# The gate chain of an RG-LRU layer in two batches of three half tiles instead of three batches of two

## The chip, the cores and the metric

The kernel runs on one core of a Trainium2 chip. The metric is the device time of one execution in microseconds (us). The kernel before took 2811.53 us, the median of three runs (2811.03 to 2813.7).

## The reference

The program is a two-layer decoder trunk in float32 for 1024 tokens of width 1024: RMSNorm, retention mixer, SwiGLU FFN, then RMSNorm, Griffin recurrent block (the LRU), SwiGLU FFN, and a final RMSNorm. The change lies wholly in the recurrent block, of width 1536 in 8 blocks of 192:

```python
gate, u = jnp.split(h @ w_in, 2, axis=-1)
u = conv4(u) + conv_b
r = jax.nn.sigmoid(einsum('bsnc,ncd->bsnd', ub, w_r) + b_r)
i = jax.nn.sigmoid(einsum('bsnc,ncd->bsnd', ub, w_i) + b_i)
log_a = (-LRU_C * softplus(-lam)) * r
a = jnp.exp(log_a)
b = jnp.sqrt(-jnp.expm1(2.0 * log_a)) * (i * u)
_, hs = lax.associative_scan(combine, (a, b), axis=1)      # hs[t] = a[t] hs[t-1] + b[t]
y = hs * jax.nn.gelu(gate)
return y @ w_out
```

## The kernel before

Each matrix product is made of three float32r products (high times high, high times low, low times high), so every operand is split: ACT (ScalarE) or POOL (GpSimd) rounds to the high part, DVE (VectorE) or POOL subtracts to get the low one. PE (TensorE) runs all products one behind the other; a 128x512 product is three matmuls per 128 rows of the contraction.

The LRU runs in four groups (g = 0 to 3) of three column tiles of 128 channels. Within a group there are six **items**: item i is tile i mod 3, half i // 3 of the 1024 tokens (512 tokens). PE makes for each item two PSUM banks, one for r and one for i (`lru_gates`, line 856 on). Tiles 0 and 2 meet two 128-row pieces of the contraction and take 6 matmuls a bank, tile 1 meets three and takes 9. PSUM has eight banks in a ring. PE waits in `free(e)` until the semaphore `psum_free` tells that bank e's last tenant is read, so DVE's count of `psum_free` sets when PE may go on.

The gate chain of a group is written out by hand for two engines:

- ACT, `gate_chain` at line 1190: `gates(i)` makes the two sigmoids out of PSUM (lines 1197 and 1202). `tanh_exp(items)` makes the tanh into `s_buf` (line 1211) and the exp, which is a, in place in `r_buf` (line 1215). `roots` takes the square root in `s_buf` (line 1221). `y_round` rounds the finished y (line 1229). Sigmoid, exp and sqrt stand in different tables, so between them ACT runs an ACT_TABLE_LOAD.
- DVE, `gate_chain` at line 1626: `gated` multiplies u by the i gate (line 1634) and is what counts `psum_free` up by two for an item. `scans` does two multiplications (1642, 1645), the scan over the tokens (1650) and the product with the gelu branch (1655). `y_split` makes the low part of y (1660).

Both go through the items in pairs: (0, 1), (2, 3), (4, 5). `s_buf` has two buffers, `r_buf` four, `i_buf` three.

What PE does right behind a group's gate products: in groups 0, 1 and 2 it is the input product of the next group. Its column tile needs two banks and is two units of 24 matmuls; the first tile wants item 2 of the group before gated, the second item 3, the third item 4. In the last group, g = 3, it is the second half (nh = 1) of group 2's output product, three units k = 0, 1, 2 of eight blocks s = 0 to 7, each block three matmuls. Blocks 0 and 1 want item 2 gated, blocks 2 and 3 item 3, blocks 4 and 5 item 4, blocks 6 and 7 item 5. Behind it comes group 3's own output product, nh = 0 first. Its unit k = 0 wants `y_ready` at 6g + 4, that is four items split, and block s of it wants DVE to have added block s of the product before to the residual (line 1353). In the last group these adds stand inside DVE's gate chain, where `meanwhile(blocks)` is called.

The bookkeeping of PE for these two places is:

```python
def lru_outof(g, u0, base, e0, nh, y_hi, y_lo):
    for k in range(GT):
        j = nh * 3 + k
        if nh == 0:
            pe.wait_ge(y_ready, g * 6 + k + 4)
        cols_unit(j, u0 + j, k, GT, y_hi, y_lo, k * S, e0, base)
```

POOL meanwhile splits weights, one unit of 128x512 at a time (`split`, lines 435, 444 and 446), each released when PE begins a unit. After the LRU come the second FFN and the end of the kernel, which take PE's whole time as well.

Of the kernel before, what the change touches and what calls it, by code (L numbers as in the profile page):

```python
# [8 lines left out]
ACT = mybir.ActivationFunctionType  # L9
# [107 lines left out]
def build(nc, x, positions, mix_norm, ffn_norm, final_norm, ret_w_in, ret_w_out, lru_w_in, lru_conv_w,  # L117
# [3 lines left out]
    with ctx:  # L121
# [110 lines left out]
        def t(i):  # L232
            return T[:, i * 512:(i + 1) * 512]

        def r3(i, n=1):
            return R3[:, i * 512:(i + n) * 512]
# [2 lines left out]
        spare = [xn[:, c:c + 512] for c in (GT * S, GT * S + 512, 4096 + GT * S)]  # L239
        r_buf = (t(0), r3(6), dk[:, 0:512], spare[0])  # L240
        i_buf = (t(1), spare[1], spare[2])
        s_buf = (r3(7), t(2))


        x_in = [sem(f"x_in{i}") for i in range(SB)]
# [657 lines left out]
        def _(act):  # L903
# [286 lines left out]
            def gate_chain(g, base, e0, y_hi):  # L1190
                def gates(i):

                    tile = i % GT
                    if i >= 4:
                        act.wait_ge(l_scan, 6 * g + i - 3)
                    full(base + e0 + 2 * i)
                    nc.scalar.activation(r_buf[i % 4], bank(e0 + 2 * i), ACT.Sigmoid,
                                         bias=gc_gate[:, 15 + tile:16 + tile]).then_inc(r_sig, 1)
                    full(base + e0 + 2 * i + 1)
                    if i >= 3:  # L1200
                        act.wait_ge(psum_free, base + e0 + 2 * i - 4)
                    nc.scalar.activation(i_buf[i % 3], bank(e0 + 2 * i + 1), ACT.Sigmoid,
                                         bias=gc_gate[:, 18 + tile:19 + tile]).then_inc(i_sig, 1)

                def tanh_exp(items):

                    for i in items:
                        if i >= 2:
                            act.wait_ge(l_scan, 6 * g + i - 1)
                        act.wait_ge(r_sig, 6 * g + i + 1)  # L1210
                        nc.scalar.activation(s_buf[i % 2], r_buf[i % 4], ACT.Tanh,
                                             scale=gc_gate[:, 21 + i % GT:22 + i % GT]).then_inc(r_tanh, 1)
                    for i in items:
                        act.wait_ge(r_tanh, 6 * g + i + 1)
                        nc.scalar.activation(r_buf[i % 4], r_buf[i % 4], ACT.Exp,
                                             scale=gc_gate[:, i % GT:i % GT + 1]).then_inc(a_exp, 1)

                def roots(items):

                    for i in items:  # L1220
                        nc.scalar.activation(s_buf[i % 2], s_buf[i % 2], ACT.Sqrt).then_inc(t_root, 1)

                def y_round(items):
                    for i in items:
                        act.wait_ge(y_out, 6 * g + i + 1)

                        act.wait_ge(psum_full, base + e0 + (6 if i < GT else 12))
                        at = i % GT * S + i // GT * 512
                        nc.scalar.activation(y_hi[:, at:at + 512], R3[:, at:at + 512], ACT.Copy)\
                            .then_inc(y_rounded, 1)  # L1230

                act.wait_ge(gc_ready, g + 1)
                gates(0)
                gates(1)
                tanh_exp((0, 1))
                roots((0, 1))
                gates(2)
                gates(3)
                y_round((0, 1))
                gates(4)  # L1240
                gates(5)
                tanh_exp((2, 3))
                roots((2, 3))
                tanh_exp((4, 5))
                y_round((2, 3))
                roots((4, 5))
                y_round((4, 5))

            u_round(0, JB_LRU, a_hi)
            gelu(0, JB_LRU, 6)  # L1250
# [26 lines left out]
        def _(dve):  # L1277
# [348 lines left out]
            def gate_chain(g, y_hi, y_lo, meanwhile=lambda blocks: None):  # L1626
# [9 lines left out]
                def scans(items):  # L1636
                    first = step.now()
                    for j, i in enumerate(items):
                        dve.wait_ge(a_exp, 6 * g + i + 1)
                        dve.wait_ge(t_root, 6 * g + i + 1)  # L1640

                        step.up(STT(s_buf[i % 2], r_buf[i % 4], 1.0, s_buf[i % 2], ALU.add, ALU.mult))
                    for j, i in enumerate(items):
                        dve.wait_ge(dve_step, first + j + 1)
                        step.up(TT(uc[:, cut(i)], uc[:, cut(i)], s_buf[i % 2], ALU.mult))
                    for j, i in enumerate(items):
                        dve.wait_ge(dve_step, first + j + 3)
                        tile, hf = i % GT, i // GT
                        start = uc[:, tile * S + 511:tile * S + 512] if hf else 0.0
                        k = nc.vector.tensor_tensor_scan(uc[:, cut(i)], r_buf[i % 4], uc[:, cut(i)], start,  # L1650
# [12 lines left out]
                link(take(gc_gate, g))  # L1663

                TS(gc_gate[:, 0:3], gc_gate[:, 21:24], -2.0, None, ALU.mult).then_inc(gc_ready, 1)
                gated((0, 1))
                scans((0, 1))
                gated((2, 3))
                y_split((0, 1))
                gated((4, 5))  # L1670
                scans((2, 3))
                meanwhile((0, 1))
                y_split((2, 3))
                meanwhile((2, 3))
                scans((4, 5))
                meanwhile((4,))
                y_split((4, 5))
                meanwhile((5, 6, 7))

            per_turn = 1 + 3 * 3 + 1 + 6 * 2  # L1680
# [88 lines left out]
```

## Time and profile before

| | |
|---|---|
| median of three runs | 2811.53 us (2811.03 to 2813.7) |
| profiled execution, its own time | 2815.13 us |
| its span, first to last instruction | 2813.3 us |
| mean granted TensorE clock | 0.985 |
| PE busy | 2712.8 us, 96% of the span |
| DVE busy | 1344.8 us, 48% |
| ACT busy | 826.1 us, 29% |
| POOL busy | 1266.7 us, 45% |
| LRU stage, about | 1595 to 2100 us of the span |
| gate chains of groups 0 to 3 on ACT and DVE, about | 1675, 1796, 1916 and 2017 us on |

Busy time is added over an engine's instructions. Matmuls overlap their neighbours: one lasts 0.39 us in the records, and the next starts 0.23 us behind it. A start time is therefore the better measure of PE's pace than a busy share. In the timeline an idle time in brackets tells what the instruction waited for.

### The profile page before, as it was taken

How to read it: one execution, taken by the hardware profiler on the slowest of the kernel's cores; microseconds unless marked ns; L12 is line 12 of the kernel's file. 1: busy time of each engine (PE TensorE's matmuls, PEld its weight loads, DVE VectorE, ACT ScalarE, POOL GpSimd, SP SyncE). 2: the span in 40 equal slices, each digit the busy share in tenths (PEclk: the TensorE clock that was granted, in tenths of full speed). 3: DMA queues.
4: the chain of work that ended last, by engine and by line, in shares of the span. 5: the costliest groups of instructions: out<-in, count | busy, mean ns of one | idle time of the engine just before them, and what ended most of it. 6: DMA issues, size and time to landing. Idle time of an engine off the chain costs nothing.

```text
span 2813.3 us, 35922 instructions
## 1 busy us (share of the span) xinstructions
PE 2712.8 (96%) x12145; PEld 2245.7 (80%) x12145; DVE 1344.8 (48%) x1854; ACT 826.1 (29%) x1398; POOL 1266.7 (45%) x1219
## 2 busy tenths in 40 slices
PE   7999999999998799999999999999987999999997
PEld 6888888888887688888888788787865888888886
DVE  7423423423424564455554636456455454545545
ACT  4220220210124423333323523415354222322223
POOL 3323323323322555665555445354335555655553
PEclk9999999999999899999999999999998999999998
DMA  3102102112111021111211111111110211111211
GB/s 132 42 27 68 40 28 68 42 31 65 45 31 49 19 64 52 52 45 52 62 54 50 36 43 53 36 53 38 38 53 16 68 52 52 45 47 56 61 52 75
DMA packets 173483, 140.06 MB, mean 50 GB/s; under 512 B 8656, under 2 KB 142928, under 8 KB 173392
## 3 DMA queue, kind: packets, MB, share of 16 engines
q1 hardware_dynamic: 171664, 133.53, 15.9%
q10 hardware_dynamic: 1728, 5.26, 0.6%
q8 instruction: 64, 1.05, 0.2%
q14 instruction: 27, 0.22, 0.0%
HBM read 133.51 MB, written 5.24 MB: 49 GB/s over the span
## 4 chain that ended last, share of the span: by engine, by line
PE 91%; DVE 4%; ACT 3%; issue 1%; POOL 1%; DMA 0%; POOLq 0%; SPq 0%; DVEq 0%; ACTq 0%
PE ps L563 30%; PE ps L566 30%; PE ps L567 30%; POOL f_h_lo L509 1%; DVE uc L1650 0%; PE ps L622 0%; DVE h_sum_a L1469 0%; DVE residual L1353 0%; ACT f_h_hi L1077 0%; DVE residual L1563 0%; DVE residual L1724 0%; ACT f_h_hi L1082 0%; PE ps L690 0%; DVE xn L1309 0%; DVE gate_buf L1655 0%
## 5 line engine op out<-in xcount | busy, mean ns | idle before, releaser
L466 POOL TENSOR_TENSOR f_w_lo<-f_raw,f_w_hi 128x512 fp32r<-128x512 f32 x263 | 341.6, 1302 | 403.8 <-ACT f_w_hi L1040 403.7
L563 PE MATMUL ps<-f_h_hi,f_w_hi 128*128 128x512 f32 x1232 | 483.7, 393 | 20.9 <-POOL f_h_lo L509 20.4
L566 PE MATMUL ps<-f_h_lo,f_w_hi 128*128 128x512 f32 x1232 | 482.4, 392 | 0.0
L567 PE MATMUL ps<-f_h_hi,f_w_lo 128*128 128x512 f32 x1232 | 482.2, 391 | 0.0
L435 POOL TENSOR_TENSOR small<-w_raw 128x1 f32<-128x1 f32 x200 | 52.7, 264 | 882.4 <-PE ps L563 867.1
L1563 DVE TENSOR_TENSOR residual<-ps,residual 128x512 f32<-128x512 f32 x352 | 239.1, 691 | 166.5 <-PE ps L567 166.5
L563 PEld LDWEIGHTS ps<-f_h_hi,f_w_hi 128*128 128x128 f32 x1232 | 233.4, 189 | 71.0 <-POOL f_h_lo L509 21.2
L563 PE MATMUL ps<-f_w_hi,f_act_hi 128*128 128x512 f32 x696 | 272.1, 391 | 6.9 <-POOL f_last_lo L466 6.9
L446 POOL TENSOR_TENSOR w_lo<-w_raw,w_hi 128x512 fp32r<-128x512 f32 x200 | 271.1, 1356 | 16.0
L1040 ACT ACTIVATE f_w_hi<-f_raw 128x512 fp32r<-128x512 f32 x263 | 165.1, 628 | 374.8 <-PE ps L567 354.3
L567 PEld LDWEIGHTS ps<-f_h_hi,f_w_lo 128*128 128x128 f32 x1232 | 233.2, 189 | 48.9
L566 PEld LDWEIGHTS ps<-f_h_lo,f_w_hi 128*128 128x128 f32 x1232 | 233.5, 190 | 48.5
L566 PE MATMUL ps<-f_w_lo,f_act_hi 128*128 128x512 f32 x696 | 271.9, 391 | 0.0
L567 PE MATMUL ps<-f_w_hi,f_act_lo 128*128 128x512 f32 x696 | 271.7, 390 | 0.0
L466 POOL TENSOR_TENSOR f_w_lo<-f_sum,f_w_hi 128x512 fp32r<-128x512 f32 x132 | 189.8, 1438 | 180.1 <-ACT f_w_hi L1040 180.1
L563 PE MATMUL ps<-h_hi,w_hi 128*128 128x512 f32 x640 | 251.3, 393 | 5.3 <-DVE uc L1634 3.2
L567 PE MATMUL ps<-h_hi,w_lo 128*128 128x512 f32 x640 | 249.5, 390 | 0.0
L566 PE MATMUL ps<-h_lo,w_hi 128*128 128x512 f32 x640 | 249.4, 390 | 0.0
L563 PE MATMUL ps<-w_hi,h_hi 128*128 128x512 f32 x560 | 219.5, 392 | 7.7 <-DVE residual L1353 6.2
L566 PE MATMUL ps<-w_lo,h_hi 128*128 128x512 f32 x560 | 218.8, 391 | 0.0
L567 PE MATMUL ps<-w_hi,h_lo 128*128 128x512 f32 x560 | 218.6, 390 | 0.0
L1518 DVE TENSOR_TENSOR gate_buf<-ps,gate_buf 128x512 f32<-128x512 f32 x132 | 91.0, 690 | 218.0 <-PE ps L567 217.3
(234 smaller groups left out, 4719.3 us busy)
## 6 DMA issues: line engine op xcount, KB each, us to landing
f_raw<-in_ffn_w_gu SPq DMA_DIRECT2D x176, 256.0 KB, 3.3
w_raw<-in_ret_w_in SPq DMA_DIRECT2D x96, 256.0 KB, 2.8
f_raw<-in_ffn_w_down SPq DMA_DIRECT2D x88, 256.0 KB, 2.8
w_raw<-in_lru_w_in SPq DMA_DIRECT2D x48, 256.0 KB, 2.9
w_raw<-in_ret_w_out SPq DMA_DIRECT2D x32, 256.0 KB, 2.6
w_raw<-in_lru_w_out SPq DMA_DIRECT2D x24, 256.0 KB, 2.7
residual<-in_x SPq DMA_DIRECT2D x8, 512.0 KB, 6.5
out_y<-residual SPq DMA_DIRECT2D x8, 512.0 KB, 2.6
```

The lines of the kernel that those rows point to most:

```text
L435: nc.gpsimd.tensor_tensor(small[:, 62:63], col, col, ALU.subtract)
L446: nc.gpsimd.tensor_tensor(lo, raw[:, cut], hi.bitcast(F32), ALU.subtract).then_inc(w_ready, 1)
L466: nc.gpsimd.tensor_tensor(lo, src, hi.bitcast(F32), ALU.subtract).then_inc(f_wready, 1)
L509: nc.gpsimd.tensor_tensor(H_lo[:, h_cut(form, k)], src[:, t_cut(k)], H_hi[:, h_cut(form, k)].bitcast(F32), ALU.subtract)\
L563: m = nc.tensor.matmul(o, l_hi, r_hi, start=start, stop=False, skip_group_check=onto)
L566: nc.tensor.matmul(o, l_hi, r_lo, start=False, stop=False, skip_group_check=onto)
L567: return nc.tensor.matmul(o, l_lo, r_hi, start=False, stop=stop, skip_group_check=onto)
L1040: nc.scalar.activation(f_unit(j, last)[0], src, ACT.Copy).then_inc(f_whi, 1)
L1518: TT(t, f_bank(u, p), t, ALU.add).then_inc(f_ev, 1)
L1563: TT(X[:, c], ps[:, b * BANK:(b + 1) * BANK], X[:, c], ALU.add).then_inc(f_ev, 1)
```

## The change

`s_buf` gets a third buffer, a new tensor of 128x512. The items go through the chain in two batches of three, (0, 1, 2) and (3, 4, 5). In the last group DVE's adds of blocks 0 to 3 stand in one place, ahead of the second batch's `scans`. PE, POOL and SP have the same instructions in the same order.

```diff
-        s_buf = (r3(7), t(2))
+        s_buf = (r3(7), t(2), sb("s_third", 512)[:])
...
                     for i in items:
-                        if i >= 2:
-                            act.wait_ge(l_scan, 6 * g + i - 1)
+                        if i >= 3:
+                            act.wait_ge(l_scan, 6 * g + i - 2)
                         act.wait_ge(r_sig, 6 * g + i + 1)
-                        nc.scalar.activation(s_buf[i % 2], r_buf[i % 4], ACT.Tanh,
+                        nc.scalar.activation(s_buf[i % 3], r_buf[i % 4], ACT.Tanh,
...
                 act.wait_ge(gc_ready, g + 1)
-                gates(0)
-                gates(1)
-                tanh_exp((0, 1))
-                roots((0, 1))
-                gates(2)
-                gates(3)
-                y_round((0, 1))
-                gates(4)
-                gates(5)
-                tanh_exp((2, 3))
-                roots((2, 3))
-                tanh_exp((4, 5))
-                y_round((2, 3))
-                roots((4, 5))
-                y_round((4, 5))
+                for i in range(3):
+                    gates(i)
+                tanh_exp((0, 1, 2))
+                roots((0, 1, 2))
+                for i in range(3, 6):
+                    gates(i)
+                y_round((0, 1, 2))
+                tanh_exp((3, 4, 5))
+                roots((3, 4, 5))
+                y_round((3, 4, 5))
...
                     for j, i in enumerate(items):
-                        dve.wait_ge(dve_step, first + j + 3)
+                        dve.wait_ge(dve_step, first + j + 4)
...
                 TS(gc_gate[:, 0:3], gc_gate[:, 21:24], -2.0, None, ALU.mult).then_inc(gc_ready, 1)
-                gated((0, 1))
-                scans((0, 1))
-                gated((2, 3))
-                y_split((0, 1))
-                gated((4, 5))
-                scans((2, 3))
-                meanwhile((0, 1))
-                y_split((2, 3))
-                meanwhile((2, 3))
-                scans((4, 5))
+                gated((0, 1, 2))
+                scans((0, 1, 2))
+                gated((3, 4, 5))
+                y_split((0, 1, 2))
+                meanwhile((0, 1, 2, 3))
+                scans((3, 4, 5))
                 meanwhile((4,))
-                y_split((4, 5))
+                y_split((3, 4, 5))
                 meanwhile((5, 6, 7))
```

On ACT, the start of the last group's chain before (`tmp` and `gate_buf` hold r and s of items 0 and 1, `decay_sb` and `xn` r of items 2 and 3; L1197 and L1202 are the sigmoids, L1211 tanh, L1215 exp, L1221 the root):

```order
L1202 ACTIVATE xn<-ps,gc_gate 128x512
L1211 ACTIVATE gate_buf<-tmp,gc_gate 128x512
L1211 ACTIVATE tmp<-gate_buf,gc_gate 128x512
L1215 ACT_TABLE_LOAD
L1215 ACTIVATE tmp<-tmp,gc_gate 128x512
L1215 ACTIVATE gate_buf<-gate_buf,gc_gate 128x512
L1221 ACT_TABLE_LOAD
L1221 ACTIVATE gate_buf<-gate_buf 128x512
L1221 ACTIVATE tmp<-tmp 128x512
L1197 ACT_TABLE_LOAD
L1197 ACTIVATE decay_sb<-ps,gc_gate 128x512
```

And in the changed kernel, where the last group's tensors are the same:

```order
L1202 ACTIVATE xn<-ps,gc_gate 128x512
L1197 ACTIVATE decay_sb<-ps,gc_gate 128x512
L1202 ACTIVATE xn<-ps,gc_gate 128x512
L1211 ACTIVATE gate_buf<-tmp,gc_gate 128x512
L1211 ACTIVATE tmp<-gate_buf,gc_gate 128x512
L1211 ACTIVATE s_third<-decay_sb,gc_gate 128x512
L1215 ACT_TABLE_LOAD
...
L1221 ACT_TABLE_LOAD
L1221 ACTIVATE gate_buf<-gate_buf 128x512
L1221 ACTIVATE tmp<-tmp 128x512
L1221 ACTIVATE s_third<-s_third 128x512
L1197 ACT_TABLE_LOAD
```

The sigmoids of item 2 now stand ahead of the first tanh, and each of tanh, exp and root has a third member. A group has six table loads where it had eight.

On DVE, the last group from the first batch's y on, before (L1634 is `gated`, L1660 `y_split`, L1353 an add of a block):

```order
L1655 TENSOR_TENSOR gate_buf<-uc,gate_buf 128x512 x2
L1634 TENSOR_TENSOR uc<-uc,xn 128x512
L1634 TENSOR_TENSOR uc<-uc,tmp 128x512
L1660 TENSOR_TENSOR h_lo<-gate_buf,h_hi 128x512 x2
L1634 TENSOR_TENSOR uc<-uc,xn 128x512 x2
L1642 SCALAR_TENSOR_TENSOR gate_buf<-decay_sb,gate_buf 128x512
...
L1655 TENSOR_TENSOR gate_buf<-uc,gate_buf 128x512 x2
L1353 TENSOR_TENSOR residual<-ps,residual 128x512 x2
L1660 TENSOR_TENSOR h_lo<-gate_buf,h_hi 128x512 x2
L1353 TENSOR_TENSOR residual<-ps,residual 128x512 x2
L1642 SCALAR_TENSOR_TENSOR gate_buf<-tmp,gate_buf 128x512
```

And changed, where the lines of DVE's code are lower by five:

```order
L1650 TENSOR_TENSOR gate_buf<-uc,gate_buf 128x512 x3
L1629 TENSOR_TENSOR uc<-uc,tmp 128x512
L1629 TENSOR_TENSOR uc<-uc,xn 128x512 x2
L1655 TENSOR_TENSOR h_lo<-gate_buf,h_hi 128x512 x3
L1348 TENSOR_TENSOR residual<-ps,residual 128x512 x4
L1637 SCALAR_TENSOR_TENSOR gate_buf<-xn,gate_buf 128x512
...
L1650 TENSOR_TENSOR gate_buf<-uc,gate_buf 128x512 x3
L1348 TENSOR_TENSOR residual<-ps,residual 128x512
L1655 TENSOR_TENSOR h_lo<-gate_buf,h_hi 128x512 x3
```

Items 3 to 5 are now gated behind a batch of three, the four adds stand together ahead of the second batch, and item 3's y is split only behind that batch.

## Rows read from the trace of the kernel before

**Rows 1.** The page, busy time of each engine
```profile
PE 2712.8 (96%) x12145; PEld 2245.7 (80%) x12145; DVE 1344.8 (48%) x1854; ACT 826.1 (29%) x1398; POOL 1266.7 (45%) x1219
```

**Rows 2.** PE's waits, 1560 to 2120 us (total us, times, longest us)
```profile
PE ps L563 <- DVE residual L1353: 6.2, 2, 6.0
PE ps L563 <- DVE uc L1634: 4.3, 4, 1.1
...
PE ps L563 <- DVE h_lo L1660: 1.5, 1, 1.5
```

**Rows 3.** PE's timeline, last group (start, duration, instruction, idle before)
```profile
2034.22 0.39 PE L567 MATMUL ps<-h_hi,wri_lo 128*128 128x512 f32 x1
2035.70 0.47 PE L563 MATMUL ps<-w_hi,a_hi 128*128 128x512 f32 x1 [1.09 <-DVE uc L1634]
...
2053.77 0.50 PE L563 MATMUL ps<-w_hi,h_hi 128*128 128x512 f32 x1 [1.47 <-DVE h_lo L1660]
...
2062.82 0.80 PE L563 MATMUL ps<-w_hi,h_hi 128*128 128x512 f32 x1 [6.03 <-DVE residual L1353]
...
2064.62 0.79 PE L563 MATMUL ps<-w_hi,h_hi 128*128 128x512 f32 x1 [0.15 <-DVE residual L1353]
...
2068.46 0.40 PE L563 MATMUL ps<-w_hi,h_hi 128*128 128x512 f32 x1
...
2073.91 0.39 PE L563 MATMUL ps<-w_hi,h_hi 128*128 128x512 f32 x1
```

**Rows 4.** Windows (length, busy of PE, PEld, DVE, ACT, POOL, granted clock, DMA)
```profile
2036.00:2042.00 6.00, 6.00 (x28) 4.94 (x27) 3.04 (x5) 5.95 (x10) 4.06 (x5) 1.00 0.11 23
...
2062.00:2069.00 7.00, 6.03 (x15) 4.30 (x16) 3.76 (x7) 1.34 (x3) 0.00 (x0) 0.55 0.71 182
```

**Rows 5.** ACT's timeline, last group, first batch
```profile
2022.41 0.69 ACT L1202 ACTIVATE xn<-ps,gc_gate 128x512 f32<-128x512 f32 x1 [1.35 <-PE ps L567]
2022.99 0.71 ACT L1211 ACTIVATE gate_buf<-tmp,gc_gate 128x512 f32<-128x512 f32 x1
2023.61 0.71 ACT L1211 ACTIVATE tmp<-gate_buf,gc_gate 128x512 f32<-128x512 f32 x1
2024.34 1.28 ACT L1215 ACT_TABLE_LOAD   x1
2025.63 0.72 ACT L1215 ACTIVATE tmp<-tmp,gc_gate 128x512 f32<-128x512 f32 x1
2026.26 0.71 ACT L1215 ACTIVATE gate_buf<-gate_buf,gc_gate 128x512 f32<-128x512 f32 x1
```

**Rows 6.** DVE's timeline, last group
```profile
2029.02 0.69 DVE L1642 SCALAR_TENSOR_TENSOR gate_buf<-tmp,gate_buf 128x512 f32<-128x512 f32 x1 [5.13 <-ACT gate_buf L1221]
...
2030.23 0.69 DVE L1645 TENSOR_TENSOR uc<-uc,gate_buf 128x512 f32<-128x512 f32 x1
...
2031.44 1.22 DVE L1650 TENSOR_TENSOR_SCAN uc<-tmp,uc 128x512 f32<-128x512 f32 x1
...
2033.69 1.26 DVE L1655 TENSOR_TENSOR gate_buf<-uc,gate_buf 128x512 f32<-128x512 f32 x2
2034.87 0.68 DVE L1634 TENSOR_TENSOR uc<-uc,xn 128x512 f32<-128x512 f32 x1
...
2048.58 2.74 DVE L1655 TENSOR_TENSOR gate_buf<-uc,gate_buf 128x512 f32<-128x512 f32 x2
...
2052.44 1.27 DVE L1660 TENSOR_TENSOR h_lo<-gate_buf,h_hi 128x512 fp32r<-128x512 f32 x2
...
2074.79 5.45 DVE L1353 TENSOR_TENSOR residual<-ps,residual 128x512 f32<-128x512 f32 x8 [9.03 <-PE ps L567]
```

**Rows 7.** POOL's timeline, weight splits in the last group
```profile
2036.32 1.70 POOL L435 TENSOR_TENSOR small<-w_raw 128x1 f32<-128x1 f32 x1 [23.69 <-PE ps L563]
...
2047.41 1.66 POOL L444 CAST w_hi<-w_raw 128x512 fp32r<-128x512 f32 x1
```

**Rows 8.** DVE's timeline, the rest of the convolution of group 1's first tile
```profile
1727.89 3.99 DVE L1610 SCALAR_TENSOR_TENSOR uc<-ps,gc_conv,uc 128x1023 f32<-128x1023 f32 x3
```

More of the change, by code:

```diff
@@ L1220, in roots @@
                     for i in items:
-                        nc.scalar.activation(s_buf[i % 2], s_buf[i % 2], ACT.Sqrt).then_inc(t_root, 1)
+                        nc.scalar.activation(s_buf[i % 3], s_buf[i % 3], ACT.Sqrt).then_inc(t_root, 1)
                 def y_round(items):
@@ L1640, in scans @@
                         dve.wait_ge(t_root, 6 * g + i + 1)
-                        step.up(STT(s_buf[i % 2], r_buf[i % 4], 1.0, s_buf[i % 2], ALU.add, ALU.mult))
+                        step.up(STT(s_buf[i % 3], r_buf[i % 4], 1.0, s_buf[i % 3], ALU.add, ALU.mult))
                     for j, i in enumerate(items):
                         dve.wait_ge(dve_step, first + j + 1)
-                        step.up(TT(uc[:, cut(i)], uc[:, cut(i)], s_buf[i % 2], ALU.mult))
+                        step.up(TT(uc[:, cut(i)], uc[:, cut(i)], s_buf[i % 3], ALU.mult))
                     for j, i in enumerate(items):
-                        dve.wait_ge(dve_step, first + j + 3)
+                        dve.wait_ge(dve_step, first + j + 4)
                         tile, hf = i % GT, i // GT
```

## The prediction

> **What bounds the kernel now.** I read the busy times first. PE works 96% of the span and the other engines less than half of it [rows 1], so the change is worth what it takes from or adds to PE's waits, and table loads saved on ACT are worth nothing by themselves. Next I read PE's waits in the LRU stage [rows 2]. Three of them belong to the gate chain. Four times, once a group, PE waits 1.1 us for a `gated` of DVE (line 1634). Once it waits 1.5 us for the split y (line 1660), and once 6.0 us for an add to the residual (line 1353), both in the last group. Last I followed the last group in the timelines of PE, ACT, DVE and POOL [rows 3, 5, 6, 7]. All times below are us of the span; where only the last group is meant I drop the leading 20, so 35.70 is 2035.70.
>
> The pace of PE: unit k = 1 starts at 68.46 and k = 2 at 73.91 [rows 3]. That is 5.44 for 24 matmuls, 0.227 a matmul, 0.68 a block of three.
>
> **Groups 0 to 2: a gain.** The last gate matmul starts at 34.22 and the next could start at 34.45, but starts at 35.70, behind item 2's `gated` at 34.87 [rows 3, 6]. That is 1.25, and with the slow first matmul behind the wait about 1.3. The three earlier groups show the same wait of 1.1 by the idle count [rows 2]. In the changed kernel items 0 to 2 are gated as soon as their sigmoids are there. Item 2's second sigmoid comes when PE has made its two banks, 12 matmuls or 2.72 behind item 1's at 22.41 [rows 5], so at 25.13, and PE wants it at 34.45. The wait goes, 3 x 1.3 = **-4.0**.
>
> What is late next is item 3's `gated`, which PE wants for the second column tile, two units later: 34.45 + 10.88 = 45.33 on the last group's clock. Below it comes out at 43.85, and a second weight split of POOL can delay it by as much as the first (1.4). That makes about 45.3, so I put **+0.3** for the three groups together (bounds: 0 if the split falls elsewhere, 3 x 1.4 = 4.2 if it costs DVE twice that). The convolution of the next group's first tile ends at 1731.9 [rows 8], while PE wants that bank 8 units behind the end of group 0's gates at about 1692.5, so at 1736.0. The changed DVE chain has the same instructions in larger batches and one idle time less, so I cost its end at nothing; if it came over 4 us later, PE would wait for it.
>
> **The last group: the first wait.** I follow the first batch. The last sigmoid moves from 22.41 to 25.13, +2.72. The third tanh costs 0.62 (22.99 to 23.61) and the third exp 0.63 (25.63 to 26.26) [rows 5]. The table loads are 1.28 each, as before. So DVE's first multiplication moves from 29.02 to 29.02 + 3.97 = 32.99. A pair then needs 1.21 for line 1642, 1.21 for line 1645, 2.25 for the scans and 1.18 for line 1655 [rows 6], so an item 0.60, 0.60, 1.13 and 0.59, and three items 8.8. Item 3's `gated` starts at 32.99 + 8.8 = 41.8 and ends 0.68 later, at 42.45.
>
> To this comes POOL. When PE begins a unit, POOL splits the next weights. DVE's pair of line 1655 took 2.74 at 48.58 beside POOL's split that has its cast at 47.41 [rows 6, 7], and 1.26 at 33.69 without them: 1.5 for one split. Here PE begins its unit at 34.45, POOL starts at about 35, and the whole split falls into DVE's multiplications and scans. At 36.32 POOL was held for 1.70 by DVE instead, and DVE lost little. Bounds are 0 and 3.0 (twice 1.5). I take 1.4, since this split too is a whole one in a busy stretch. Item 3 is gated at 43.85.
>
> The Trainium skill (GPSIMD Engine Reference, Specifications) says that GpSimd's SBUF interfaces are shared with VectorE and that contention comes with VectorE instructions that read two SBUF inputs. By that the adds, which read one input from PSUM, should not be slowed, while every step of `scans` may be. With no such effect the sum would be 1.4 lower.
>
> Blocks 0 and 1 of PE's unit run at once, and block 2, due at 34.45 + 1.36 = 35.81, starts at 43.85 + 0.15 = 44.0, where the 0.15 is the distance from the end of `gated` (35.55) to the matmul at 35.70. **PE waits 8.2 where it waited 1.25.** The clock then falls. The granted clock stayed at 1.00 (2.4 GHz) around the wait of 1.09, and was 0.55 on the mean in the 7 us around the wait of 6.03 [rows 4], that is 1.2 GHz for most of it. There 12 matmuls took from 62.82 to 68.46, 5.64, with a late start of 0.35 inside (the 0.15 of idle time at 64.62 [rows 3]). Against 2.72 that is 2.57 lost. I take the same here. Bounds: 0 if the clock holds, 3.6 if all 18 matmuls left of the unit run at half speed (18 x 0.2).
>
> **The last group: the second wait.** DVE's order is now `gated` 3 to 5, three splits, adds 0 to 3, and then the second batch. ACT rounds item 2's y until about 44, then three tanh, a load, three exp and a load take 1.9 + 1.3 + 1.9 + 1.3, so the roots come at about 51 and 52, and it is the adds that decide. From 44.0 PE needs 18 blocks until block 3 of unit k = 2 is full: 12.24 - 0.23 + 2.57, and 0.43 from the last matmul's start to the add (that distance at 74.79: the block's third matmul starts 0.45 behind 73.91 [rows 3, 6]). So add 3 starts at 59.0. Then 0.6 for it, 7.0 for three items up to line 1655, 1.8 for three of line 1655, 0.6 for add 4, and 0.68 + 0.06 for item 3's split, the fourth that `y_ready` wants (the pair at 52.44 ends at 53.71 and PE starts at 53.77 [rows 3, 6]): 69.75. POOL is quiet in this stretch. Before, PE's unit k = 0 started at 53.77 and had done four of its eight blocks ahead of its wait of 6.03, since it needed only items 0 to 3. Now PE stands from about 61.5 to 69.8, and all eight blocks are left. The clock is lost here as it was before. The unit ends at 69.8 + 5.29 + 2.72 = 77.8, where it ended at 68.46: **+9.4**. This holds the loss of the first wait and the gain of this group's own 1.3.
>
> Behind this unit everything hangs on PE as before: adds 5 to 7 start at 71.5 at the latest, about when block 5 is due at the slow pace. The second FFN's preparation waits for PE and POOL and moves with them.
>
> **Sum.** -4.0 + 0.3 + 9.4 = **+5.7**. Against the profiled execution (2815.13, span 2813.3) that is 2820.8. That execution lies 3.6 above the median of the three runs, and the difference carries over, so I forecast 2811.5 + 5.7 = **2817.2**. What a measurement of this kernel can tell from no change is about 0.2%, 5.6, and the forecast lies on that bound.
>
> **Rivals.**
>
> - *The clock holds in the first wait, or POOL costs nothing there.* The one gives 5.7 - 2.6 = +3.1 (2814.6), the other 5.7 - 1.4 = +4.3 (2815.8). For it speaks that DVE lost little to the split at 36.32. Against it speaks that 6.03 was enough for the clock to fall, and 6.8 is left even without POOL. Both are not slower. Chance 0.24.
> - *Gain: the table loads are the bound.* ACT loses 2 of 8 loads a group, 8 x 1.28 = 10.3, and the kernel would be at 2801.2. It decides from the point where PE waits for the end of ACT's chain in each group. The Trainium skill (ScalarE: Activation LUTs, Table sets) asks to batch by set and puts a switch at about 2.66, which would make 21 of it. The rows show a load of 1.28 with nothing behind it [rows 5], and PE waits in groups 0 to 2 for 1.1 alone [rows 2], which bounds the gain at 4.0 there. It also needs PE's two waits in the last group not to grow. Chance 0.06, with all other ways to a gain.
> - *Item 3 is late in groups 0 to 2 as well.* Two weight splits in the first batch cost DVE up to 1.4 a group more than I take: +4.2, so 2821.4. For it: the second split begins with PE's second unit, at 39.9, just ahead of that `gated`. Against it: DVE and POOL do not lose each time they meet. Chance 0.10.
>
> **How the numbers follow.** The forecast has 0.60. Its own range is about 2.5 either way (clock 1.2, POOL 1, the rest of the reckoning 1), 2814.7 to 2819.7, with 0.42 of it above 5.6 and 0.18 below. Slower by over 0.2%: 0.42 + 0.10 = 0.52. Within 0.2%: 0.18 + 0.24 = 0.42. Faster: 0.06. The range takes in the clock that holds and most of the late item 3: 2813.5 to 2821.
>
> **What would show it.** Right: PE's three waits for `gated` behind groups 0 to 2 are gone. In the last group there are two waits, of about 8 us each, the first for `gated` of item 3 (line 1629 there), the second for item 3's split y (line 1655), each followed by half a dozen us of half clock. DVE stands idle before its four adds, with ACT's roots long done. Wrong: a first wait under 7, a clock of 1.00 behind it, a wait at the second column tile of groups 1 to 3, or a second batch in the last group that waits for ACT and not for the adds.

## Result and profile after

The changed kernel takes 2818.51 us (median of 16 runs, 2817.82 to 2820.46). The kernel before, timed in the same rounds, takes 2812.62 (16 runs, 2811.03 to 2814.41). The ratio is 1.0022, with a 95% interval of 1.0014 to 1.0029: **5.9 us slower**, where +5.7 was forecast. In us the interval is about 4 to 8. One execution of all that are timed in this document, of the kernel with threes in groups 0 to 2 only, took 5550.16 us where the others of that kernel took 2807 to 2810, and it is left out of that kernel's median.

The single profiled executions lie closer together: 2815.13 before, 2818.31 after, or +3.2. That is because the profiled execution of before ran 2.2 us late when its last transposes of line 622 began (1614.9 against 1612.7), ahead of all four gate chains. So I measure the stage by its own length, from there to the last transpose of line 750. This is 513.0 us before and 518.6 after, **+5.6**, and it is the length meant by "stage" below. It holds nearly all of the difference between the medians.

The busy times of the page, against [rows 1]:

```profile
PE 2712.8 (96%) x12145; PEld 2245.4 (80%) x12145; DVE 1357.1 (48%) x1854; ACT 816.5 (29%) x1390; POOL 1263.7 (45%) x1219
```

PE's busy time is the same to a tenth. ACT has 8 instructions and 9.6 us less, two table loads a group. DVE has the same 1854 instructions and 12 us more, 10.6 of them in the stretch of groups 0 to 2. Where single rows are read below, POOL's work beside DVE is what makes them longer; for all 12 us this is not shown. None of these sums tells that the kernel is slower. PE's waits do (total us, times, longest), against [rows 2]:

```profile
PE ps L563 <- DVE h_lo L1655: 8.2, 1, 8.2
PE ps L563 <- DVE uc L1629: 8.0, 1, 8.0
...
PE ps L563 <- DVE a_lo L1619: 2.6, 2, 1.3
```

The four waits of 1.1 for `gated` have become one of 8.0, in the last group. The waits of 6.0 for an add and of 1.5 for a split have become one of 8.2 for a split. The third row was 2.6 before as well. PE's timeline of the last group (start, duration, instruction, idle before), against [rows 3]:

```profile
2029.28 0.39 PE L563 MATMUL ps<-w_hi,a_hi 128*128 128x512 f32 x1
...
2038.79 0.79 PE L563 MATMUL ps<-w_hi,a_hi 128*128 128x512 f32 x1 [7.99 <-DVE uc L1629]
...
2044.07 0.44 PE L563 MATMUL ps<-w_hi,a_hi 128*128 128x512 f32 x1
...
2064.77 0.80 PE L563 MATMUL ps<-w_hi,h_hi 128*128 128x512 f32 x1 [8.21 <-DVE h_lo L1655]
...
2068.46 0.40 PE L563 MATMUL ps<-w_hi,h_hi 128*128 128x512 f32 x1
...
2071.87 0.39 PE L563 MATMUL ps<-w_hi,h_hi 128*128 128x512 f32 x1
```

The first row answers to "could start at 34.45" of before, so subtracting leads to a common frame: this kernel is 5.17 earlier there. The 12 matmuls from 2038.79 to 2044.07 take 5.28 instead of 2.72, so 2.56 are lost to the clock. The 9 from 2064.77 to 2068.46 take 3.69 instead of 2.04, 1.65 lost. The unit k = 1 begins at 2071.87, 42.59 behind the end of the gates. Before, it was 68.46 - 34.45 = 34.01. **The last group loses 8.6.**

The granted clock in the windows around both waits (length, busy of PE, PEld, DVE, ACT and POOL, clock, DMA), against [rows 4]:

```profile
2037.00:2045.00 8.00, 6.21 (x16) 4.91 (x17) 4.75 (x8) 7.95 (x11) 0.00 (x0) 0.55 0.00 0
2063.00:2070.00 7.00, 5.23 (x16) 4.22 (x17) 4.72 (x8) 1.18 (x2) 2.08 (x3) 0.64 0.15 39
```

DVE's timeline shows what PE waited for, against [rows 6]:

```profile
2027.80 0.69 DVE L1637 SCALAR_TENSOR_TENSOR gate_buf<-tmp,gate_buf 128x512 f32<-128x512 f32 x1 [6.35 <-ACT gate_buf L1221]
...
2030.82 1.10 DVE L1640 TENSOR_TENSOR uc<-uc,s_third 128x512 f32<-128x512 f32 x1
2031.84 2.27 DVE L1645 TENSOR_TENSOR_SCAN uc<-tmp,uc 128x512 f32<-128x512 f32 x1
2034.04 1.19 DVE L1645 TENSOR_TENSOR_SCAN uc<-gate_buf,uc 128x512 f32<-128x512 f32 x1
...
2036.27 1.86 DVE L1650 TENSOR_TENSOR gate_buf<-uc,gate_buf 128x512 f32<-128x512 f32 x3
2038.06 0.68 DVE L1629 TENSOR_TENSOR uc<-uc,tmp 128x512 f32<-128x512 f32 x1
...
2051.84 2.73 DVE L1348 TENSOR_TENSOR residual<-ps,residual 128x512 f32<-128x512 f32 x4 [10.10 <-PE ps L567]
2054.49 0.68 DVE L1637 SCALAR_TENSOR_TENSOR gate_buf<-xn,gate_buf 128x512 f32<-128x512 f32 x1
...
2061.64 1.88 DVE L1650 TENSOR_TENSOR gate_buf<-uc,gate_buf 128x512 f32<-128x512 f32 x3
...
2064.03 1.89 DVE L1655 TENSOR_TENSOR h_lo<-gate_buf,h_hi 128x512 fp32r<-128x512 f32 x3
```

Two things are to be seen. The bank that PE wants is freed by the row at 2038.06, which stands behind three whole items of the first batch. And at 2051.84 DVE had stood idle for 10.10 us, waiting for PE to fill banks that its four adds want; only then does the second batch begin, at 2054.49. ACT's timeline shows that the roots for it had long been there:

```profile
2045.21 0.63 ACT L1221 ACTIVATE gate_buf<-gate_buf 128x512 f32<-128x512 f32 x1
...
2062.35 1.83 ACT L1229 ACTIVATE h_hi<-gate_buf 128x512 fp32r<-128x512 f32 x3 [15.47 <-DVE gate_buf L1650]
```

The three roots end at about 2046.9, 7.6 us ahead of their use. PE waits for DVE, DVE waits for PE, and the second batch sits between. The other part, POOL's weight split beside the first batch, against [rows 7]:

```profile
2030.29 1.08 POOL L444 CAST w_hi<-w_raw 128x512 fp32r<-128x512 f32 x1
2031.45 1.58 POOL L446 TENSOR_TENSOR w_lo<-w_raw,w_hi 128x512 fp32r<-128x512 f32 x1
```

Beside the cast, DVE's multiplication takes 1.02 from start to start (2030.82 to 2031.84) where it takes 0.60 alone. Beside the subtraction, the scan takes 2.20 (2031.84 to 2034.04) instead of 1.13. Together that is 1.5 us for one weight split.

### The profile page after: what moved, and what is told of

The parts are those of the page before. It is cut to its first block, busy times and chain, and to the rows that moved or that the text cites. A ratio compares the mean times of both kernels' runs of the same rounds, so it can differ in the third digit from the quotient of the medians.

```text
span 2816.5 us, 35912 instructions
## 1 busy us (share of the span) xinstructions
PE 2712.8 (96%) x12145; PEld 2245.4 (80%) x12145; DVE 1357.1 (48%) x1854; ACT 816.5 (29%) x1390; POOL 1263.7 (45%) x1219
## 4 chain that ended last, share of the span: by engine, by line
PE 92%; DVE 3%; ACT 2%; issue 1%; POOL 1%; DMA 0%; POOLq 0%; SPq 0%; DVEq 0%; ACTq 0%
PE ps L563 31%; PE ps L566 30%; PE ps L567 30%; POOL f_h_lo L509 1%; PE ps L622 0%; DVE h_sum_a L1464 0%; DVE residual L1348 0%; DVE residual L1558 0%; DVE residual L1715 0%; ACT f_h_hi L1077 0%; PE ps L690 0%; ACT f_h_hi L1082 0%; DMA residual<-in_x 0%; DVE xn L1304 0%; ACT gate_buf L909 0%
```

## The experiments

Times are medians. The kernels were timed in three sets, each beside runs of the kernel before, whose medians were 2812.70 (28 runs, for the first four rows below the changed kernel), 2812.86 (33 runs, for the next four) and 2812.62 (26 runs, for the last three). Each kernel ran 11 times unless another number stands. An interval of the ratio is about 2.5 us wide to either side, so differences of 1 or 2 us between two medians are inside it; the stage and PE's waits, from one profiled execution each, tell the finer differences.

| run | us | ratio to before (95%) | stage |
|---|---|---|---|
| changed kernel | 2818.51 | 1.0022 (1.0014 to 1.0029) | 518.6 |
| threes in groups 0 to 2 only (10 runs) | 2808.28 | 0.9984 (0.9974 to 0.9993) | 509.3 |
| threes in the last group only (6 runs) | 2821.42 | 1.0031 (1.0019 to 1.0043) | 521.8 |
| adds behind the second batch | 2813.90 | 1.0004 (0.9995 to 1.0014) | 512.6 |
| pairs, with the third buffer | 2812.35 | 1.0000 (0.9991 to 1.0009) | 513.0 |
| gated items 3 to 5 early | 2812.29 | 0.9997 (0.9988 to 1.0006) | 511.9 |
| both of these | 2813.47 | 1.0001 (0.9992 to 1.0010) | 513.0 |
| two loads more, each group | 2819.57 | 1.0024 (1.0015 to 1.0033) | 519.8 |
| item 3 alone first | 2812.08 | 0.9998 (0.9989 to 1.0008) | 511.5 |
| two loads more, last group (10 runs) | 2818.51 | 1.0023 (1.0013 to 1.0032) | 518.7 |
| item by item in the last group | 2806.78 | 0.9980 (0.9971 to 0.9989) | 506.0 |
| item 3 first, last group only | 2807.88 | 0.9987 (0.9978 to 0.9996) | 508.4 |

### Where the gain and the loss lie: one kind of group at a time

A flag of `gate_chain` picks the order of before (pairs, two root buffers) or of the change. First, the last group is put back into pairs:

```diff
-            gate_chain(GROUPS - 1, h_hi, h_lo, second_half_out)
+            gate_chain(GROUPS - 1, h_hi, h_lo, True, second_half_out)
```

> Groups 0 to 2 in two batches of three, the last group in pairs as before. My theory (the loss is in the last group alone, the three others gain about 1.0 us each): 3.0 us under the kernel before, so a ratio of 0.9989, and no wait over 1.3 us on PE behind groups 0 to 2. A rival, that each group pays the same for its batches of three and the last one is not special: between the kernel before and the changed one, about +1.5 to +4 us. A second rival, that the eight table loads saved count: six of them are saved here, 7.7 us under the kernel before.

Measured: 2808.28, 4.4 below the kernel before, with an interval of about 2 to 7. Equal shares, which would have made it slower, are refuted; 7.7 for the saved loads lies just outside. The second kernel is its mirror image: pairs in groups 0 to 2, threes in the last.

> Groups 0 to 2 in pairs as before, only the last group in two batches of three. My theory: +8.6 us against the kernel before (ratio 1.0031), made of a first wait of PE of 8 us, a second of 8 us and a second stretch at half clock. The rival of equal shares: +1.5 to +2 us. The four waits of 1.1 us for the gate product shall be there behind groups 0 to 2.

Measured: 2821.42, 8.7 above. PE's waits of the one and of the other:

```profile
PE ps L563 <- DVE residual L1367: 6.2, 2, 6.0
...
PE ps L563 <- DVE h_lo L1676: 1.5, 1, 1.5
PE ps L563 <- DVE uc L1650: 1.1, 1, 1.1
```

```profile
PE ps L563 <- DVE uc L1650: 11.2, 4, 8.0
PE ps L563 <- DVE h_lo L1676: 8.2, 1, 8.2
```

Three waits of 1.1 are gone from the first kernel, and the last group's waits are those of before. The second has the three waits and the two long ones of the changed kernel. So the change is a gain of about 4 in three groups and a loss of about 9 in one. The two add up to +4.3 by the medians and to +5.1 by the stages, against +5.9 and +5.6 for the whole change: inside the intervals.

### Is it the third buffer?

The kernel before gets the third root buffer and keeps its order in pairs. The edit is against the kernel before, and every `s_buf[i % 2]` becomes `s_buf[i % 3]`:

```diff
-        s_buf = (r3(7), t(2))
+        s_buf = (r3(7), t(2), sb("s_third", 512)[:])
...
-                        if i >= 2:
-                            act.wait_ge(l_scan, 6 * g + i - 1)
+                        if i >= 3:
+                            act.wait_ge(l_scan, 6 * g + i - 2)
...
```

> The order in pairs of the kernel before, with the third root buffer alone. My theory: the tanh of item 4 no longer waits for a scan on ScalarE (2.0 us), but nothing on PE waits for it, since the last pair on VectorE stands behind the adds: within 0.5 us of the kernel before. The rival, that the wait for a root buffer was on the path: up to 3 us under it.

Measured: 2812.35 against 2812.70, with PE's waits as before. The buffer by itself does nothing that can be measured; the effect is that of the order.

### The second wait: do the adds hold the second batch?

```diff
                 y_split((0, 1, 2))
-                meanwhile((0, 1, 2, 3))
                 scans((3, 4, 5))
-                meanwhile((4,))
                 y_split((3, 4, 5))
-                meanwhile((5, 6, 7))
+                meanwhile(range(SB))
```

> The changed kernel, but in the last group all eight adds of the residual stand behind the second batch and its splits. My theory (the second batch waits for the adds, and they wait for PE, which was late from its first wait): VectorE starts the second batch when the roots are there, about 8 us earlier, and the split of item 3 is done about when PE ends the product before. PE's second wait falls from 8.2 to 1 or 2 us and its clock stays at 1.00 there, so 8 to 9 us under the changed kernel, or 3 us under the kernel before. The rival, that the batch of three itself is too long for PE whatever stands ahead of it: the second wait stays over 5 us and the time within 3 us of the changed kernel.

Measured: 2813.90, 4.6 below the changed kernel, where 8 to 9 had been expected. PE's waits, and the window of the second:

```profile
PE ps L563 <- DVE uc L1629: 8.0, 1, 8.0
...
PE ps L563 <- DVE residual L1348: 3.5, 1, 3.5
```

```profile
2060.00:2067.00 7.00, 6.31 (x28) 5.28 (x29) 4.73 (x8) 0.00 (x0) 2.29 (x5) 1.00 0.32 84
```

The wait of 8.2 is gone, and one of 3.5 for the adds, now late, stands in its place; behind it the clock stays at 1.00. The second batch begins at 2046.22 instead of 2054.49, as soon as the roots are there. That settles what held it, and the rival's wait of over 5 did not come. The size was off, since I had moved the batch out of POOL's quiet stretch. DVE's timeline:

```profile
2048.46 1.77 DVE L1640 TENSOR_TENSOR uc<-uc,gate_buf 128x512 f32<-128x512 f32 x1
...
2055.21 2.92 DVE L1650 TENSOR_TENSOR gate_buf<-uc,gate_buf 128x512 f32<-128x512 f32 x3
```

The first takes 0.6 without POOL beside it, the second 1.88 (row at 2061.64 above). Two weight splits of POOL now meet the batch and cost some 3 us together: from its first instruction to the end of its last line 1650 the batch takes 11.8 us (2046.22 to 2058.06) where it took 8.9 (2054.49 to 2063.43).

### The first wait: does `gated` 3 stand behind too much?

`gated` of items 3 and 4 is issued behind the multiplications, and of item 5 behind the first scan. For that ACT must not be held either: in the changed kernel its sigmoid of item 4 waits for a scan to free `r_buf` (11.6 us of idle time in all, by the groups of ACT's lines), so `r_buf` gets six buffers:

```profile
L1197 ACT ACTIVATE tmp<-ps,gc_gate 128x512 f32<-128x512 f32 x7 | 4.8, 688 | 11.7 <-DVE uc L1645 11.6
```

```diff
-        r_buf = (t(0), r3(6), dk[:, 0:512], spare[0])
+        r_more = sb("r_more", 1024)
+        r_buf = (t(0), r3(6), dk[:, 0:512], spare[0], r_more[:, 0:512], r_more[:, 512:1024])
...
-                    if i >= 4:
-                        act.wait_ge(l_scan, 6 * g + i - 3)
...
-                scans((0, 1, 2))
-                gated((3, 4, 5))
+                scans((0, 1, 2), (3, 4), (5,))
```

> The changed kernel with six buffers for r instead of four, and on VectorE the gate products of items 3 and 4 ahead of the first batch's scans and that of item 5 behind the first of them. My theory: PE's first wait in the last group falls from 8.0 us to about 2 and its clock stays at 1.00 there; the adds come 8 us earlier, so the second batch starts when its roots are there, about 6.5 us earlier than in the changed kernel, and PE's second wait grows to about 10. The late gate product behind groups 0 to 2 (0.3 us each) goes as well. About 7 us under the changed kernel, 2811.5. The rival, that the first wait is no cause of the second: only the first wait and its clock are won on PE and the second stays at 8, 10 us and more under the changed kernel.

Measured: 2812.29, 6.2 below the changed kernel. PE's waits:

```profile
PE ps L564 <- DVE h_lo L1658: 8.2, 1, 8.2
...
PE ps L564 <- DVE uc L1628: 2.8, 1, 2.8
```

The first wait fell from 8.0 to 2.8. What is left of it is the six multiplications behind the roots, and POOL's split beside them and beside `gated` 3, which takes 1.5:

```profile
2029.36 1.10 DVE L1639 TENSOR_TENSOR uc<-uc,s_third 128x512 f32<-128x512 f32 x1
2030.38 1.75 DVE L1628 TENSOR_TENSOR uc<-uc,tmp 128x512 f32<-128x512 f32 x1
```

The second stayed at 8.2, where about 10 had been expected: the batch is tied to the adds, and the adds to PE, so an earlier PE brings everything forward together. In this the rival was right, but its 10 us and more did not come; the time is near my 2811.5. There was a surprise behind the 2.8, taken up in the last section.

With both edits together:

> Both: the early gate products, and the eight adds of the last group behind the second batch. My theory is that with the adds out of the way the chain of ScalarE and VectorE ends at the same time whatever PE's first wait was, so what the first wait gives back the second takes: the time of the run with the adds behind, within 1.5 us (2813), a first wait of 2 us and a second of 10 to 11 with the slow clock behind it. The rival, that the two gains add up: 5 us and more under either.

Measured: 2813.47, as expected. PE's wait for the adds is now 10.9. The edits alone gain 4.6 and 6.2 on the changed kernel, and both together only 5.0: with the PE that comes earlier and eight adds at the end, the one wait takes what the other gave.

### Is ACT the bound?

The changed kernel saves 8 table loads. If ACT's chain set the pace, two loads more in each group would take the saving back or worse. Two one-column activations do that, ahead of the second roots:

```diff
                 tanh_exp((3, 4, 5))
+                if True:
+                    nc.scalar.activation(small[:, 60:61], ident[:, 0:1], ACT.Sqrt)
+                    nc.scalar.activation(small[:, 61:62], ident[:, 0:1], ACT.Exp)
                 roots((3, 4, 5))
```

> The changed kernel with two table loads more in the second batch of each group, between exp and roots (two activations of one column each, 2.9 us in all a group), so with the number of loads of the kernel before. My theory: in the last group nothing, since VectorE stands 10 us before its adds there. In groups 0 to 2 the convolution of the next group's first tile ends at 1733.9, just when PE wants its bank (1734.2), so a chain that is 2.9 us later costs PE 2 to 3 us a group: 6 to 9 us over the changed kernel. If that bank has more room than I think, 0; if every load is on the path, 11 to 12 us.

Measured: 2819.57, 1.1 above the changed kernel; a miss, for my theory too. This execution ran 0.3 late at the end of group 0's gates. Against that the roots came 3.0 later, but the convolution behind them began only 0.5 later (1729.30 against 1728.49), since the shifted batch met less of POOL's work: it took 17.1 us (1711.91 to 1728.98) where it had taken 19.6 (1708.58 to 1728.17). PE lost 0.2 to 0.35 a group (in one, its matmul started at 1734.80 where 1734.61 was due), which is most of the 1.2 by the stage. That all loads count, which would make 11 to 12, is refuted. The same in the last group alone:

> The changed kernel with two table loads more in the last group's second batch alone. My theory: the roots come 3 us later and VectorE, which stands 10 us before its adds, takes them 4 us after that: the time of the changed kernel within 1 us. If table loads are on the path, 3 us more.

Measured: 2818.51, the time of the changed kernel to the hundredth, which is chance; the stage is 518.7 against 518.6. The roots began at 2047.40 there, 3.0 later against the end of PE's gates, and were used at 2053.73: the 3 us went into ACT's slack. The Trainium skill (ScalarE: Activation LUTs, Table sets) asks to batch activations by their table set. Here that removed 8 loads, and putting 8 back cost 1.2 us by the stage, none of it in the last group; so they were worth 1 us or so, not their 10.3.

### A version that beats both

What the runs so far ask for in the last group: begin the second batch as soon as the roots are there, but let no piece of work stand ahead of what PE wants next. PE's unit k reads tile k alone, that is items k and k + 3, so unit k = 0 needs only items 0 and 3. The first version therefore takes items 3 to 5 through the multiplications, then item 3 alone to its end, and puts adds and splits between the rest (all on top of the early gates). PE waits for two splits per tile:

```diff
-                        pe.wait_ge(y_ready, g * 6 + k + 4)
+                        pe.wait_ge(y_ready, g * 6 + (2 * k + 2 if y_hi is h_hi else k + 4))
...
-                y_round((0, 1, 2))
                 tanh_exp((3, 4, 5))
                 roots((3, 4, 5))
-                y_round((3, 4, 5))
+                y_round((0, 1, 2, 3, 4, 5))
...
+                scan_y(3)
+                meanwhile((0, 1))
+                y_split((0, 3))
+                meanwhile((2, 3))
+                scan_y(4)
                 meanwhile((4,))
+                y_split((1,))
+                meanwhile((5,))
+                y_split((4,))
+                meanwhile((6, 7))
+                scan_y(5)
+                y_split((2, 5))
```

> The early gate products; ScalarE rounds all y behind the roots; in the last group VectorE brings item 3 through first, the adds stand between the items in the order in which PE wants them, and PE's output product waits for the splits of the pairs (0, 3), (1, 4), (2, 5) in this order. My theory: the roots come 1 us earlier, item 3 is split about 7 us behind the first root, PE's second wait is 3 to 5 us with no or little slow clock. 12 to 16 us under the changed kernel and 7 to 10 us under the kernel before (2803 to 2806). If VectorE's own work is the bound instead, the waits of PE for items 4 and 5 grow to over 3 us together and the gain is under 6 us.

Measured: 2812.08, a miss by 6 and more. PE's waits name two causes:

```profile
PE ps L564 <- DVE h_lo L1657: 4.7, 1, 4.7
...
PE ps L564 <- DVE uc L1603: 2.5, 3, 0.9
```

The second row is the convolution in groups 1 to 3. I had moved the roundings of y behind the roots in every group, so the splits of items 0 to 2 came late there, and the convolution behind them. And behind the 4.7 the clock fell. The next kernel keeps the early roundings in groups 0 to 2 (against the kernel just shown):

```diff
+                if y_hi is not h_hi:
+                    y_round((0, 1, 2))
                 tanh_exp((3, 4, 5))
                 roots((3, 4, 5))
-                y_round((0, 1, 2, 3, 4, 5))
+                if y_hi is h_hi:
+                    y_round((0, 1, 2))
+                y_round((3, 4, 5))
```

> The last group just as in the run with item 3 first, groups 0 to 2 as in the run with the early gate products. My theory: the three waits of 0.7 to 0.9 us for the convolution, which came because the splits of items 0 to 2 stood behind the roots, go, and nothing else changes: 3 us under the run with item 3 first (2809), a second wait of 4.7 us in the last group with slow clock behind it. If the last group's new order was the cause of the missing gain, no change.

Measured: 2807.88. The row of line 1603 is gone, which shows that cause; 4.7 stands. The gain was 4.2 (3.1 by the stage) where 3 had been expected, and the slow clock behind the 4.7 was shorter in this execution, 7 matmuls instead of 13. The last version carries item 3, then 4, then 5 each through all four operations, with adds and splits between them. PE's edit is that of the run with item 3 first, and the lines that go are left out here:

```diff
+                through(3)
+                y_split((0,))
+                meanwhile((0,))
+                y_split((3,))
+                meanwhile((1, 2, 3, 4, 5))
+                through(4)
+                y_split((1,))
+                meanwhile((6, 7))
+                y_split((4,))
+                through(5)
+                y_split((2, 5))
```

> Groups 0 to 2 as in the run with the early gate products; the last group as in the run with item 3 first, but VectorE takes items 3, 4 and 5 through one by one, each with all its steps, so item 3 is split 2.4 us earlier. My theory: no wait for the convolution in groups 1 to 3 (they were 2.5 us), PE's second wait about 2.5 us with the clock staying at 1.00, then one more wait of 2 to 3 us for item 4. 6 to 8 us under the kernel before (2805 to 2807). If VectorE's total work is the bound, the waits only move from one place to the other and it stays at 2808 to 2810.

Measured: **2806.78**, 5.8 below the kernel before and 11.7 below the changed one. PE's waits in the LRU's last group, and the clock in the stretch that holds the last two:

```profile
PE ps L564 <- DVE residual L1350: 3.2, 1, 3.2
...
PE ps L564 <- DVE uc L1631: 2.8, 1, 2.8
...
PE ps L564 <- DVE h_lo L1661: 1.8, 1, 1.8
```

```profile
2048.00:2062.00 14.00, 8.98 (x39) 6.83 (x38) 13.79 (x21) 1.26 (x2) 4.20 (x6) 1.00 0.57 158
```

One wait of 8.2 has become waits of 1.8 and 3.2, and the clock is 1.00 throughout. DVE is busy for 13.79 of these 14 us. So DVE is probably the bound there now; whether yet another order of the same work would gain more was not tried. (One detail was off: the 3.2 stands at an add queued behind item 4, where I had named item 4 itself.)

## Why the prediction was right, and where its terms were off

- **Groups 0 to 2, -4.0 and +0.3.** The three waits went, as said. From the last transposes of line 622 to the end of the last group's gates it is 419.55 us before (1614.90 to 2034.45) and 416.58 after (1612.70 to 2029.28), a gain of 3.0, not 3.7. The term that was too small is the late item 3. The second weight split did meet DVE there (line 1650 at 1697.38 takes 3.38 for three where 1.86 is usual), so item 3's `gated` ends 11.0 behind the end of the gates (1690.36 to 1701.36), where the forecast had 10.8. The forecast also left out the 0.15 from the end of `gated` to PE's matmul, which it counted in the last group, and the slow first matmuls. PE's second column tile starts right behind item 3's `gated`, at 1701.49 where 1701.24 was due, and slow, which makes about 0.35 a group and 1.0 in three:

```profile
1700.68 0.68 DVE L1629 TENSOR_TENSOR uc<-uc,tmp 128x512 f32<-128x512 f32 x1
```

```profile
1701.49 0.49 PE L563 MATMUL ps<-h_hi,w_hi 128*128 128x512 f32 x1
```

- **The convolution, costed at nothing.** The time was right, the reason was not. I had put its cover at 4 us. In the changed kernel it ends at 1733.85, and PE takes the bank at 1734.28 without a wait:

```profile
1729.87 3.98 DVE L1605 SCALAR_TENSOR_TENSOR uc<-ps,gc_conv,uc 128x1023 f32<-128x1023 f32 x3
```

The cover is 0.43, or 0.3 if the 0.15 from a bank's release to the matmul is taken off. "Larger batches and one idle time less" left out that the second batch begins later, behind three `gated`, three splits and later roots, and meets a weight split of POOL. Both kernels that delayed it a little more (two loads more; item 3 first) got waits there at once. By my estimate from these rows, a batch 1 us longer would have cost PE 0.7 in each of three groups, and the forecast would have been 2 too low. That it was not is luck.
- **The first wait, 8.2.** It is 8.0. In before's frame `gated` 3 ends at 43.91 (forecast 43.85), and the clock cost 2.56 (forecast 2.57). POOL's share was 1.5 where 1.4 was taken. The run with the early gates shows that the place in DVE's order is the cause.
- **The second wait.** It is 8.2, and PE resumes at 69.94 in before's frame (forecast 69.75). That the adds decide and not ACT is shown from both sides: with the adds moved, the batch starts 8 us earlier; with the roots 3 us later in the last group, nothing happens. The mis-sized term is the clock behind this wait: 1.65 instead of the same loss as before, 2.57. So the last group cost **+8.6** and not +9.4. This term is not a fixed one. Behind the same wait of 8.2 the slow clock cost 1.6 to 1.9 in four of the profiled executions and 2.8 in that with threes in the last group only.
- **The sum.** -3.0 + 8.6 = +5.6, with +5.6 by the stage and +5.9 by the medians. Two errors of 0.7 and 0.8 cancelled, and that the sum comes out to a tenth is luck: the clock alone can move it by 1. The absolute forecast of 2817.2 is 1.3 too low, 1.1 of it because the kernel before came out at 2812.62 with 16 runs and not at the 2811.53 of the first three.
- **The rivals.** The clock did not hold in either wait, and POOL did cost. The slow stretches lasted 5.3 and 3.7 us, where half a dozen had been said. The loads as bound are refuted. Item 3 late in the earlier groups is true in kind, at 0.35 a group instead of up to 1.4.

## What to carry to other kernels

A larger batch saves on one engine what each batch costs, but all that stands behind it in the order comes later by the size of what was added. Before batching, list what the waiting engine wants next and look where each of these stands: here one `gated` of 0.68 us behind three items, and one batch behind four adds that wait for PE themselves. Where two engines wait for each other, breaking the work at the pieces the other wants first, with the gate products early, gained twice as much on the changed kernel as the change had lost. And where a change is good in the steady groups and bad in the last, keep it for those alone (-4.4 against +5.9 here).

## What the runs showed of the hardware

**The clock behind a wait.** Behind PE's waits of 10.9, 8.2, 8.0, 6.0 and 4.7 us in the last group the granted clock fell to half in every profiled execution: starts are 0.43 apart instead of 0.23, for some 3 to 6 us. The loss differs from one execution to the next behind the same wait. It was 1.9 to 3.0 us behind the 8.0, and 1.6 to 2.8 behind the 8.2. Behind waits of 3.5, 3.2 and 1.8 the clock stayed at 1.00. The wait of 2.84 stands in five of the kernels, all with the gates early. In the other four the clock stayed at 1.00 behind it; in the run with the early gates alone it fell, and PE's timeline shows the slow part only from the seventh matmul behind the wait on, from 2033.68 to 2037.32: 3.64 us for 9 matmuls instead of 2.04:

```profile
2032.19 0.50 PE L564 MATMUL ps<-w_hi,a_hi 128*128 128x512 f32 x1 [2.84 <-DVE uc L1628]
...
2033.68 0.59 PE L564 MATMUL ps<-w_hi,a_hi 128*128 128x512 f32 x1
2034.07 0.63 PE L567 MATMUL ps<-w_lo,a_hi 128*128 128x512 f32 x1
2034.49 0.63 PE L568 MATMUL ps<-w_hi,a_lo 128*128 128x512 f32 x1
...
2037.32 0.40 PE L564 MATMUL ps<-w_hi,a_hi 128*128 128x512 f32 x1
```

In the item-by-item version the same wait, at 2033.06, is followed by none, with a clock of 1.00 from 2033 to 2041. What decides there stays open, and so does how often the 1.6 us are lost in the executions without a profile.

**POOL beside DVE.** A weight split of POOL (cast and subtraction, 2.7 us) costs DVE 1.5 us where DVE works from SBUF on both inputs, and POOL is slowed in turn (its cast takes 0.61 alone, took 1.08 above and 1.66 in [rows 7]). The adds, with one input in PSUM, were not slowed, and neither was POOL. In the item-by-item kernel five adds took their usual 0.6 each beside a whole split:

```profile
2050.01 3.07 DVE L1350 TENSOR_TENSOR residual<-ps,residual 128x512 f32<-128x512 f32 x5
```

```profile
2050.92 0.61 POOL L445 CAST w_hi<-w_raw 128x512 fp32r<-128x512 f32 x1
2051.61 1.29 POOL L447 TENSOR_TENSOR w_lo<-w_raw,w_hi 128x512 fp32r<-128x512 f32 x1
```

The Trainium skill (GPSIMD Engine Reference, Specifications) speaks of shared interfaces and of contention for instructions with two SBUF inputs; the rows here agree, and put a price on it. In this kernel the price fell on the early batch and not on the late one, which is why moving the adds behind gained 4.6 (6.0 by the stage) and not 8.

**Table loads.** A load takes 1.28 us and the activation behind it starts within 0.02 us of its end. Eight more in the whole kernel cost 1.1 us, and two more in the last group nothing.
